# A one-core decoder trunk on Trainium2: five reorderings of its queues, with two norms cut into halves

## The reference, cut to what is computed

```python
h = rmsnorm(x, g1) * (1 + scale1(c)) + shift1(c)      # scale, shift, gate: silu(c) @ ada_w
p = h @ w_in          # columns for three groups of heads
# NSA, 8 query heads, 2 kv heads: compressed, selected and window attention, mixed by sigmoid gates;
#   a sample token sees 2048 cached tokens in pages, and a window of 512
# mLSTM, 4 heads: matrix memory C and normaliser n with gates and a running maximum
# pool, 4 groups: trailing means over 2/4/8/16 tokens minus the token, a linear map, a scale
x = x + gate1(c) * (concat(nsa, mlstm, pool) @ w_out)
h = rmsnorm(x, g2) * (1 + scale2(c)) + shift2(c)
a, b = split(conv3(h @ w_up))
x = x + gate2(c) * ((silu(a) * b) @ w_down)
y = rmsnorm(x, gf)
```

## Time and profile before

| | before |
|---|---|
| median of 3 runs | 835.34 us (834.02 to 838.09) |
| the profiled execution | 837.06 us, of which the span of the trace is 835.3 us |
| PE busy | 769.3 us (92%) |
| DVE busy | 517.0 us (62%) |
| ACT busy | 329.0 us (39%) |
| POOL busy | 308.9 us (37%) |
| mean granted clock | 0.968 |
| chain that ended last | PE 68%, DVE 15%, DMA 5%, issue 4%, SP's queue 4% |

### The profile page before, as it was taken

The page is one execution under the profiler, slowest core; times in us unless marked ns, Lnnn a source line. Parts: engine busy times, 40 slices in busy tenths (PEclk is TensorE's granted clock), DMA queues, the critical chain, the costliest instruction groups (busy, mean ns, idle before and its releaser), DMA issues.

```text
span 835.3 us, 18836 instructions
## 1 busy us (share of the span) xinstructions
PE 769.3 (92%) x7509; PEld 709.8 (85%) x7509; DVE 517.0 (62%) x1027; ACT 329.0 (39%) x601; POOL 308.9 (37%) x163
## 2 busy tenths in 40 slices
PE   2899989999997979989969999999999999999993
PEld 2798979988875646669969999999999999999993
DVE  3745799995868778754675666664123666665324
ACT  3432222333431646652245545443123554544221
POOL 0042656672000424443323344343443434434340
PEclk9999999999986989999999999999999999999997
DMA  9964777788895354342611333332223333232312
GB/s 338 341 237 133 232 233 260 246 287 266 314 315 145 102 184 126 74 153 103 269 51 64 123 111 109 126 105 98 79 100 112 104 126 98 93 101 76 102 46 102
DMA packets 73143, 131.24 MB, mean 157 GB/s; under 512 B 12685, under 2 KB 47389, under 8 KB 72929
## 3 DMA queue, kind: packets, MB, share of 16 engines
q1 hardware_dynamic: 68656, 120.62, 43.7%
q10 hardware_dynamic: 4368, 9.44, 3.3%
q0 software_dynamic: 32, 0.00, 0.0%
HBM read 124.56 MB, written 9.12 MB: 160 GB/s over the span
## 4 chain that ended last, share of the span: by engine, by line
PE 68%; DVE 15%; DMA 5%; issue 4%; SPq 4%; ACT 2%; POOL 1%; DVEq 0%; ACTq 0%; POOLq 0%
PE ps L677 54%; PE ps L1063 2%; PE ps L1041 2%; PE ps L1026 2%; DVE arena L1529 2%; SPq L530 2%; PE ps L1079 1%; DMA arena<-cache_keys 1%; DVE arena L1530 1%; DVE arena L1526 1%; DMA raw<-weights 1%; DMA arena<-weights 1%; PE ps L931 1%; DMA out_pool<-arena 1%; DVE arena L2144 1%
## 5 line engine op out<-in xcount | busy, mean ns | idle before, releaser
L677 PE MATMUL ps<-hR,wR 128*128 128x260 f32 x3456 | 429.3, 286 | 9.5 <-ACT hR L1169 4.3
L677 PEld LDWEIGHTS ps<-hR,wR 128*128 128x128 f32 x3456 | 422.8, 191 | 13.9 <-issue 8.6
L640 POOL TENSOR_TENSOR wR<-raw,wR 128x1024 fp32r<-128x1024 f32 x92 | 225.8, 2455 | 300.3 <-ACT wR L1161 300.3
L1161 ACT ACTIVATE wR<-raw 128x1024 fp32r<-128x1024 f32 x94 | 99.4, 1057 | 215.2 <-PE ps L677 208.3
L677 PE MATMUL ps<-fR,wR 128*128 128x260 f32 x1056 | 128.1, 283 | 2.2 <-DVE fR L2115 2.0
L677 PEld LDWEIGHTS ps<-fR,wR 128*128 128x128 f32 x1056 | 127.0, 188 | 3.1 <-DVE fR L2115 2.4
L2139 DVE COPY arena<-arena 128x2 f32<-128x2 f32 x44 | 47.6, 1082 | 93.6 <-ACT arena L1452 93.6
L633 POOL TENSOR_SCALAR arena<-arena,fac 128x128 f32<-128x128 f32 (+3 forms) x32 | 40.4, 1264 | 127.1 <-DVE fac L2038 127.1
L621 POOL TENSOR_TENSOR arena<-arena,par 128x512 f32<-128x512 f32 x32 | 42.6, 1332 | 75.9 <-DMA arena<-cache_keys 74.5
L2100 DVE TENSOR_TENSOR t<-ps,mod 128x8 f32<-128x8 f32 x24 | 4.0, 167 | 107.3 <-PE ps L677 107.3
L1385 ACT ACTIVATE arena<-ps,nmx 128x128 f32<-128x128 f32 (+3 forms) x64 | 33.1, 524 | 24.5 <-DVE nmx L2029 24.4
(11 more groups left out here) (368 smaller groups left out, 827.2 us busy)
## 6 DMA issues: line engine op xcount, KB each, us to landing
raw<-weights SPq DMA_DIRECT2D x104, 512.0 KB, 3.6
arena<-cache_keys SPq DMA_DIRECT2D x128, 192.0 KB, 3.4
arena<-weights SPq DMA_DIRECT2D x30, 512.0 KB, 8.8
arena<-cache_values SPq DMA_DIRECT2D x128, 64.0 KB, 2.0
x<-xT SPq DMA_DIRECT2D x16, 260.0 KB, 4.2
arena<-weights ACTq DMA_DIRECT2D x6, 512.0 KB, 6.1
out_y<-x SPq DMA_DIRECT2D x8, 260.0 KB, 2.5
arena<-win_values SPq DMA_DIRECT2D x8, 256.0 KB, 3.2
```

Source lines behind the costliest of these rows:

```text
L640: nc.gpsimd.tensor_tensor(w_slot(i)[:, 1, :, :], raw[:, g % RAW, :, :], w_slot(i)[:, 0, :, :].bitcast(F32), ALU.subtract).then_inc(lo_read ...
L677: last = mm(ps[:, a + half, 0:TH], w_slot(i)[:, wp, k, :], src[:, hp, j, half * TH:(half + 1) * TH], start=(j == 0 and q == 0), stop=(j == ...
L1161: A(w_slot(i)[:, 0, :, :], raw[:, g % RAW, :, :], ACT.Identity).then_inc(hi_ready, 1)
```

## The change

Five edits, none of which adds or drops a product. One: `wq` is made inside the product of the gate rows, behind its sixth chunk, and the mLSTM gate rows come first among DVE's work between the halves (with "rows" at p = 8 on ACT); the trailing sums are cut in two steps and spread out. Two: the sample tokens' mLSTM state work goes to units 18 to 26, and SP's list of loads and stores from 227 us on is put in another order. Three: `pooled_mix` and `across` go ahead of the last triple; the scaling of the sample weights and `pooled_result` go from DVE to ACT; `mod` is added ahead of the gate product, and unit 0 waits for `mod`, in banks 2 and 3, and unit 1 for `mmix_ready`, in banks 0 and 1. Four: the output product takes the rows of `mix` in the order 6, 7, 4, 5, 0 to 3. Five: the last output product and the last down product run one half of the columns after the other, and the norm behind each is done by halves, the final stores too.

```diff
@@ events: wq and rows
-        if t == 3:
-            pend.append(("q",))
-        if p == 10:
+        if p == 8:
             out.append(("rows",))
...
+                    for j in range(KD):
+                        chunk(n, j)
+                        if (n, j) == (IN_AT[3] + 1, 5):
+                            key_queries()
@@ DVE between the halves
-                if h in (1, 3):
-                    trailing_sums(h // 2)
-                elif h in (2, 4):
-                    trailing_means(h // 2 - 1)
-                elif h == 5:
+                if h == 1:
                     gate_rows()
+                elif h in (2, 5):
+                    trailing_sums(h // 5)
+                elif h in (3, 9):
+                    trailing_differences(h // 9)
+                elif h in (4, 10):
+                    trailing_means(h // 10)
+                elif h == 6:
+                    gate_sums()
                 elif h == 7:
-                    gate_sums()
+                    gate_maxima()
                 elif h == 8:
-                    gate_maxima()
-                elif h == 9:
                     gate_copies()
-                elif 10 <= h < 14:
-                    prompt_sums((h - 10) // 2, h % 2)
+                elif 11 <= h < 15:
+                    prompt_sums((h - 11) // 2, (h - 11) % 2)
@@ SP from 227 us on
             load_values(0)
-            sp.wait_ge(slot_done, N_A + 6 * RAW)
-            load_values(1)
-            sp.dma_start(cst[:, :], mC).then_inc(rec_landed, 16)
+            raw_wait(sp, N_A + 8 * RAW - 1)
             sp.dma_start(o_fm, pT[:, T_KC:T_MK, 0:S]).then_inc(early_out, 16)
             sp.dma_start(o_vn, vn[:, :, :]).then_inc(early_out, 16)
+            sp.dma_start(o_pool, pT[:, T_PU:T_PU + 2, S - 15:S]).then_inc(early_out, 16)
+            sp.dma_start(o_st, sT[:, :, :]).then_inc(early_out, 16)
+            sp.dma_start(o_snv, sn[0:NB, 7 * P:9 * P]).then_inc(early_out, 16)
+            load_values(1)
             sp.wait_ge(slot_done, len(PART1))
             sp.wait_ge(mmix_ready, 1)
             load_window(0)
             load_window(1)
+            sp.dma_start(cst[:, :], mC).then_inc(rec_landed, 16)
+            sp.wait_ge(early_out, 16 * 5)
+            load_values(2)
+            sp.wait_ge(spv_done, 1)
+            load_window(2)
+            load_values(3)
+            sp.wait_ge(spv_done, 2)
+            load_window(3)
+            for g in range(len(PART1), len(PART1) + RAW):
+                load_slot(g)
+            load_values(4)
+            load_values(5)
             sp.wait_ge(pool_ready, 1)
...
-            sp.wait_ge(early_out, 16 * 5)
-            load_values(2)
-            load_values(3)
-            for g in range(len(PART1), len(PART1) + RAW):
-                load_slot(g)
-            for b in range(2, NB):
+            for b in range(4, NB):
                 sp.wait_ge(spv_done, b - 1)
                 load_window(b)
                 if b + 2 < NB:
                     load_values(b + 2)
@@ PE, end of stage 3
             inside(3)
-            triple(7)
+            pooled_mix()
             across(2)
             across(3)
+            triple(7)
             triple_turn(5)
-            pooled_mix()
@@ state work of the sample tokens between the units
-                elif k == 11:
+                elif k == 18:
                     state_products()
-                elif k == 13:
+                elif k == 20:
                     state_output()
-                elif k == 16:
+                elif k == 22:
                     state_rows()
-                elif k == 17:
+                elif k == 24:
                     state_outer()
-                elif k == 18:
+                elif k == 26:
                     state_new()
@@ output product
+        MIX_ORDER = [6, 7, 4, 5, 0, 1, 2, 3]
-            pe.wait_ge(mix_ready, 1)
@@ PE, last out and last down1 product
+            def product_halves(n, norm):
+                for half in range(2):
+                    for j in range(chunks):
+                        if half and norm == 2 and j == chunks - 5:
+                            norm_half(norm, 0)
...
+                    if half == 0:
+                        last.then_inc(half_done, 1)
@@ DVE, final norm
-            add_squares(2, KD - 1)
-            root(2)
-            for k in range(KD):
-                V.scalar_tensor_tensor(x[:, k, :], x[:, k, :], par_("gf", k, k + 1), rstd[:, :], ALU.mult, ALU.mult)\
-                    .then_inc(out_ready, 1)
+            add_squares(2, KD - 2)
+            residual_half(len(PART2) - 1, 40, 2, 0)
+            add_half(2, 0)
+            residual_half(len(PART2) - 1, 40, 2, 1)
+            root(2, 0)
+            final(0, 0).then_inc(out_ready, 1)
+            add_half(2, 1)
+            for k in range(1, KD):
+                final(k, 0).then_inc(out_ready, 1)
+            root(2, 1)
             for k in range(KD):
+                final(k, 1).then_inc(out_ready, 1)
```

More of the change, by code:

```diff
@@ L1343, in triple_read, with samples_scale, pooled_result @@
                         load_weights(BEFORE.index(n))
+            def samples_scale(r, buf):
+                act.wait_ge(sx_in, 4 + r)
+                A(buf, buf, ACT.Identity, scale=ssx[:, 12 + r:13 + r]).then_inc(sp_ready, 1)
+            def pooled_result():
+                act.wait_ge(pool_mm, 1)
+                for t in range(2):
+                    A(mix[:, 6 + t, 0:S], ps[:, 4 + t, :], ACT.Identity, scale=par_("pool_s", t, t + 1))
+                    A(mix[:, 6 + t, S:T], ps[:, 7, t * NB:(t + 1) * NB], ACT.Identity, scale=par_("pool_s", t, t + 1))
             weights(0)
@@ L1417, in _ @@
                     nhi += 1
-                if kind == "out" or kind == "up":
+                if kind == "up" or kind == "out" and t < KD - 1:
                     item_ready(act, n)
@@ L2086, in _ @@
             last.then_inc(mix_ready, 1)
-            for k in range(KD):
-                dve.wait_ge(h_hi, KD + k + 1)
-                V.tensor_tensor(hR[:, 1, k, :], mix[:, k, :], hR[:, 0, k, :].bitcast(F32), ALU.subtract).then_inc(h_lo, 1)
+            for j in range(2, KD):
+                mix_low(j)
             def residual(m, gate, done):
@@ L2120, in _ @@
                         dve.wait_ge(x_landed, 32 * KD)
-                    residual(m, 16, t + 1)
-                    if t >= 2:
-                        add_squares(1, t - 1)
+                    if t < KD - 1:
+                        residual(m, 16, t + 1)
+                        if t >= 2:
+                            add_squares(1, t - 1)
                     if t == KD - 1:
-                        add_squares(1, KD - 1)
-                        root(1)
+                        add_squares(1, KD - 2)
+                        for h in range(2):
+                            residual_half(m, 16, 1, h)
+                            add_half(1, h)
+                        root(1, 1)
                         normed(1, "g2", 32, 24)
```

217 lines of the change are left out of this document (145 added, 72 removed).

## The result

| | before | after |
|---|---|---|
| median of 20 runs | 836.12 us (829.90 to 840.25) | 831.52 us (825.73 to 837.97) |
| the profiled execution | 837.06 us, span 835.3 | 827.82 us, span 826.0 |
| mean granted clock in it | 0.968 | 0.974 |
| PE busy, DVE busy | 769.3, 517.0 us | 764.7, 516.5 us |

The ratio is 0.9947, with a 95% interval of 0.9923 to 0.9971: 4.4 us faster, where 27.8 were forecast. The change is faster, but by a sixth of what I said, and the time lies outside my range.

The account below looks back on a forecast made before the run. PE, 92% busy, was taken as the bound, with gains where it stands still or runs at half clock. Eight terms sum to 27.8 us off 837.06, 809.3; against the median, 807.5 us; range 800 to 821.

Parts of the forecast that it names:

- Query product: Input products: `wq` two chunks earlier shortens PE's wait for `qw` by 1.4 us, plus 1.5 of clock; 2.9 us.
- DVE's order: Input products: half 4 ends sooner, so PE's 3.31 us stall at half 6 and the clock behind it go; 4.0 us.
- the rival: DVE bounds the input products: PE trades the stall at half 6 for stalls at halves 9 to 13; 811.5 us, chance 0.10.
- Triples: SP's values wait until ACT's last weight slot landed: 1.3 us of PE's weight waits and 1.5 of clock go; 2.8 us.
- Start of the units: PE's 2.51 us wait for gate product L1962 goes, less 0.40 for unit 0's mask; 2.1 us.
- Loads in the units: Sample 2's window wait and its clock go, 7.2 us, less 0.5 for window 4 and 1.1 for state work; 5.6 us.
- SP is late: Rival: SP is late with one or two windows in the units; 815 to 822 us, chance 0.07.
- Output product: PE's wait ahead of it shrinks by 2.3 us and 3.7 us of clock come back; 6.0 us.
- Second norm: Behind the output product: the first half's square, sum, matmul and root run beside PE's second half; 1.4 us.
- Final norm: Behind PE's last down product: by halves, the first eight final products run inside the second half's chain; 3.0 us.
- 11 us of clock: Clock gains over five places, 10.8 to 11 us; rival that the clock does not come back: 818.5 us, chance 0.18.

Follow-up runs that it names:

- e13: e11 with DVE's gate sums, maxima and copies moved behind halves 9 to 11, and the second pair's sums, differences and means behind half 15; 818.5 us.
- e4: The changed kernel with SP's list in triples and units as before the change, only the last state stores left at the end; 827.0 us, ratio 0.9919.
- e12: e10 with the blocks of mix in plain order 0 to 7, behind all copies; 830.0 us, ratio 0.9932.
- e10: The changed kernel with loads by need, stores as in e9, weight slots sooner, state's products at unit 21, second norm in one piece; 827.0 us.
- e5: The changed kernel with only the pooled, C and m stores moved from ahead of window 4 to behind window 5 and values 7; 831.1 us, ratio 0.9951.
- e3: The changed kernel with SP's loads of the units in the order of need; 821.9 us, ratio 0.9836.
- e9: The changed kernel with only the pooled, C and m stores moved from ahead of window 4 to right behind windows 0 and 1; 826.9 us, ratio 0.9893.
- e11: e10 with the second norm by halves, as in the change; 824.4 us, ratio 0.9884.
- e2: The changed kernel with sample 1's sixteen value transfers moved from ahead of windows 0 and 1 to behind them; 835.7 us, ratio 0.9984.
- e8: e3 with DVE's steps between the halves and the gate rows' place as before the change; 822.3 us, ratio 0.9862.

## Why the prediction was wrong, step by step

**Query product** (2.9): right; 3.1 us here, and the stretch is 16.1 or 16.2 us in every kernel with the change against 19.3.

**DVE's order** (4.0): the step "DVE's total work is the same ... I take off 0.6" failed. The stall at half 6 went to halves 9 to 14, as the rival said. But the rival's reason, that DVE is full, fell too: e13 removes the stall with the same instructions. What counted was the work that stood behind halves 5 to 8, the gate steps (3.29 us the longest) and the second pair's sums, though e13 doesn't part the two. That DVE's work stays the same was wrong in itself: its time depends on where it stands, 97.5 us or 103.9. I had worked out page arrivals "within 0 to 2 us of PE's need", and priced that at 0.6; the runs of this order show 4.1 us of idle time of PE in the stage.

**Triples** (2.8): right in the table by luck, for a wrong reason. The waits on weights stayed, 1.8 us against 1.7, though SP issued no values of sample 1 then, and e4 with the old list takes 49.0 us against the change's 48.8. What differed was the clock, and that is not the change's doing. The stretch takes 48.5 to 56.4 us in the thirteen profiles of kernels with the change. Two of them, e12 and e10, have the same instructions there. e12 by stretches:

```profile
201.20:249.80 48.60, 46.83 (x689) 38.75 (x689) 39.36 (x102) 22.33 (x57) 0.00 (x0) 1.00 0.85 307
```

e10, and its slow part alone:

```profile
206.20:262.60 56.40, 55.84 (x689) 46.53 (x689) 39.25 (x103) 22.39 (x57) 0.00 (x0) 0.82 0.72 255
222.00:243.00 21.00, 21.00 (x209) 17.57 (x211) 9.31 (x26) 5.50 (x16) 0.00 (x0) 0.53 0.54 177
```

7.8 us from the clock, and PE shows no gap from 208 us on, where it fell at about 223.5. I had tied every fall of the clock to a gap ahead of it; the 3 us of the earlier trace rows at 246 us were not the change's to win. The Trainium skill, "TensorE: Matmul & The Clock Gate", section "What's actually happening", which I had drawn on for a part of the clock that can change for no reason in the kernel, says that the ramp up to full clock varies from run to run. The two executions here differ too, but in a fall to the lower level under a busy PE, for which that statement does not speak.

**Start of the units** (2.1): right; 2.6 here, 1.7 to 2.6 in the others (the stretch takes 1.0 to 1.9 us against 3.6). The 0.4 us that I took off for the masks is there as well: the next stretch, to sample 0's values, takes 12.0 us in most of them against 11.6.

**Loads in the units** (5.6): wrong, by 13.7 us, and most of the error. The step that failed was "window 4 stands behind 32 value transfers, the pool and state stores and three slots; at 0.6 us a transfer (19.24/32) it lands about when PE [...] wants it. I take off 0.5". I charged the stores their issue time, 2.8 us, and not their transfer: the window behind them is used 8.2 us after its issue, where in e5, without them, it was there within 3.0. Its issue came late as well, though less: the 32 values took 0.68 us each (21.87/32), 2.6 us more in all, and PE was ready 14.5 us ahead of the old time (326.33 less 311.80), not 12. In the kernel before the same four stores went out at 263.90 to 269.34 us, and the next window only at 293.77, so its trace had no window behind them to show the price. The rival "SP is late" was named, at 0.07, without that cause. The state's work costs 1.7 us at unit 18, taken at 1.1.

**Output product** (6.0): the wait went, 2.5 us. Of the clock I counted 3.7; the product takes 46.5 us here and in e3, e9, e10 and e11 (its first 42 us at 1.00), but 47.7 to 47.9 in e2, e4 to e8 and e13 (at 0.96), against 49.1 in the one profile of before. So 1.2 to 2.6 us, and 3.7 to 5.1 in all. How much of it is the change's is not shown: e12, with the old order and the old wait, takes 47.9 too.

**Second norm** (1.4): the step "halving lets the first half's square, sum, matmul and root run beside PE's second half" failed, for the reasons shown above: the first half starts late beside POOL, its matmul stands behind the second half in PE's list, and the 0.4 us that is left goes in `normed`'s first operation. Nil.

**Final norm** (3.0): right, 3.3. At this place POOL is idle (its last operation ends at 807.0) and the matmul stands five chunks ahead of the end. The stores keep DVE's pace, as did those of the earlier trace rows; DVE's row after:

```profile
817.12 6.09 DVE L2286 SCALAR_TENSOR_TENSOR x<-x,par,rstd 128x260 f32<-128x260 f32 x15
```

**The sum, done again.** With what several traces show instead of one, and the output product near its lower end: 3.1 + 0 + 0 + 2.6 + 0 + 3.8 + 0 + 3.3 = 12.8 us if the units break even (14.1 with its upper end). In e9, without the stores' harm, the runs lie 8 to 9 us below those of before; the rest of 4 to 5 us is about what is left of waits in its units (3.2 us for ACT at the first weight slot, 1.7 for `pcT`), though no run took both away alone, so this last step is argued; e10 and e11, which took the first away and moved the second, are no faster than e3. The four stores take another 4.6 in the changed kernel. Of the 11 us of clock in my forecast, the query product's 1.5 came back in every profile (that stretch is at 1.00) and at most 2.6 of the output product's 3.7; the triples' 1.5 goes with the execution. Over the 80 runs of before in these comparisons the time ranges from 829.3 to 847.1 us and goes with the mean clock (0.971 and 0.952 at the two ends).

## What to carry to other kernels

Price a store that is put ahead of a load by its transfer in its real pieces, not by its issue, and ask how long ahead of need the load behind it goes out: here a window behind the four stores needed some 8 us, and 11.1 us of lead was free where 0.7 cost 6.9. A stall that leaves one place has to be looked for at every later place where the two engines meet, and an estimated lead of "0 to 2 us" there has to be priced as a stall. Work of one engine takes longer in one place than in another, so moving it changes its sum too. Low clock behind a gap is only to be counted as a gain where several executions show it at the same place.

## What the runs showed of the hardware

Identical instructions took 48.6 us in one execution and 56.4 in another: in the longer one the granted clock fell to its lower level for about 20 us, with PE busy throughout. A DVE sum of two SBUF operands of 520 columns took 0.70 us alone and 2.92 beside a 2.40 us POOL operation. The first operation of `normed` on DVE, small as it is, took 0.23 us alone and 1.12 beside such an operation. A 256 KB window behind four small-piece stores landed 7.6 to 8.2 us after its issue, and within 3.0 us with the stores elsewhere.
